# Where three stage seams of a two-layer decoder trunk norm and transpose their tiles, on eight cores

## The chip, the cores and the metric

The kernel runs on the 8 NeuronCores of one Trainium2 chip. Each core computes two of the 16 sequences, and the cores exchange nothing. A core has TensorE (PE, matrix products and transposes into PSUM), VectorE (DVE), ScalarE (ACT), GpSimd (POOL) and a sync engine (SP), each with a queue of its own that runs in program order; semaphores order them against each other. The metric is the device time of the slowest core in microseconds.

## The reference

The reference computes a trunk of two layers over `x` (16 x 2048 x 1024). Cut to what is computed:

```python
for i in range(2):
    h = rms_norm(x, mix_norm_g[i])
    # layer 0: gMLP gating + stick-breaking attention; layer 1: retention, 4 heads
    x = x + (hybrid_sg_sb_mixer(h, ...) if i % 2 == 0 else retention_mixer(h, ...))
    x = x + conv_ffn(rms_norm(x, ffn_norm_g[i]), ffn_w_up[i], ffn_conv_w[i], ffn_conv_b[i], ffn_w_down[i])
    gate = sigmoid(rms_norm(x, ple_norm_g[i]) @ ple_w_gate[i])
    x = x + gate * rms_norm(p[i] @ ple_w_proj[i], ple_post_g[i])
return rms_norm(x, final_norm_g)
# conv_ffn: a = h @ w_up; causal depthwise conv of width 3 over positions; (gelu(gate) * up) @ w_down
```

## The kernel before

A core keeps the residual stream X of one sequence in SBUF, as 16 tiles of 128 tokens by 1024, and runs six stages over it for each of its two sequences: mixer 0, FFN 0, embedding stage 0 (the gate with `p`, called PLE in the code), mixer 1 (retention), FFN 1, embedding stage 1, which is also the final norm and writes the output ("final stages" below).

**Norming a tile** has two halves. `norm_h` (L449, ACT) copies a tile of X, scaled by its reciprocal root mean square, to a bf16 buffer. `norm_tr` transposes it in 8 pieces of 128 x 128 on TensorE into one PSUM bank (L458), and DVE multiplies it by the gain and writes it to SBUF (L462, "gain multiply"). `norm_hT2` does both. The statistics come from `stat_tile`: a Square with accumulation on ACT (L435) and two small operations on POOL (L429, L431).

**FFN** (`phase_ffn_ple`, L1081 ff.). The up product runs over 22 column chunks, and each chunk over five stretches of 410 tokens; one such item has 16 matmuls (L1168) into two of six PSUM banks, two ACT copies (L1174, L1176), four conv steps on DVE (L1178 to L1185), a Gelu on ACT (L1182) and a product on POOL (L1187). In front of an item `make_ht` norms all tiles up to three beyond those that the item reads, with two buffers and banks 6 and 7 in turn. So seven tiles are normed before item 0, and three before each of the items 1, 2 and 3. The down product of each quarter of the chunks is spread over the items of the next quarter (L1134, added to X by DVE in L1141, "adds"); the last quarter's goes into the embedding stage.

**Embedding stage.** The loop over `m` runs 16 + 7 times. An iteration issues, for tile m-1, `norm_tr`; for m, the last down product (10 matmuls into banks 6 and 7); for m-3, `act_gate` (Square over the projection L1278, Sigmoid of the gate L1280), POOL's statistics, the embedding multiply on DVE (`u_of`, L1283) and POOL's product (`prod`, L1288); for m the adds and `stat_tile`; for m-4 the residual update on DVE (`xfin`, L1238) and the Square of the result (L435; L1246 in final stages); in final stages for m-6 the output (L1251); for m-2 the gate product (L1263, 16 matmuls, banks 2 and 3) and the projection (L1271, 4 matmuls, banks 4 and 5); for m `norm_h`. Iterations 16 to 22 drain the loop. The scheduler lets no second engine read a PSUM bank before the first reader has finished with it, so L1283 waits for L1278.

**Retention** (`phase_mix1`). Four heads with 16 steps each. A step of `stage_a` has the q/k product (L1421, 32 matmuls), four rotary multiplies on DVE (L1430) and POOL's sums (L1433, L1434); L1451 is the v and gate product, L1525 the transposes of the head's output Y. Before step 0, DVE scales four pieces of the output weights (L1380) and the tiles 0 and 1 are normed with one buffer; in head 0, step i norms tile i+2, with bank 3.

**Order and memory.** Nothing reorders work: each engine runs its instructions as the Python code emits them. The scheduler (`Sched.add`) only puts in the waits that reads and writes need. SBUF is one arena, and a buffer placed over old ones waits for all their readers and writers.

## Time and profile before

| | before |
|---|---|
| median of 3 runs | 5250.73 us (5227.94 to 5593.7) |
| profiled execution | 5247.87 us, its span on the slowest core 5246.0 us |
| spans of the other cores | 5203.1 to 5232.6 us |
| mean granted TensorE clock, core 0 | 0.940 |
| PE, DVE, ACT, POOL busy | 84%, 61%, 47%, 29% of the span |

The run of 5593.7 us was disturbed; the two others and the profiled one are comparable. In timelines, a row gives the start and the length in us, the engine, the line of the kernel, the operation with destination and source, how many there are, and in brackets how long the engine stood before it and what ended that. PE rows come from a pipelined engine, so the lengths of neighbouring rows overlap a little. The granted clock is given in parts of 2.4 GHz; 0.5 is 1.2 GHz.

### The profile page before, as it was taken

Reading aid. Unit: us, or ns where it says so; the run is one execution under the profiler, and the core shown is the slowest. Engines: PE = TensorE matmul, PEld = TensorE weight load, DVE = VectorE, ACT = ScalarE, POOL = GpSimd, SP = SyncE. Lnnn points to the kernel's source line nnn. Section 1 sums busy time; section 2 is a strip of 40 time slices with the busy share of each in tenths; the row PEclk is TensorE's granted clock in tenths of the full one; section 3 lists DMA queues with packets and bytes.
Section 4 is the critical chain, followed back from the end, with each engine's and each line's share of the span. In section 5 each row is a group of like instructions: output and inputs, shape, how many; then the busy total and the mean of one; then the engine's idle time right before and its main releaser. Section 6 shows DMA issues by size and latency. Waiting matters only on the chain.

```text
span 5246.0 us, 78294 instructions; the slowest of 8 cores (5203.1 to 5246.0 us)
## 1 busy us (share of the span) xinstructions
PE 4428.8 (84%) x25713; PEld 2227.8 (42%) x26098; DVE 3188.2 (61%) x5552; ACT 2474.1 (47%) x3578; POOL 1505.9 (29%) x1899
## 2 busy tenths in 40 slices
PE   4887789987789897998758877899878889889986
PEld 2322245543445454554323222455435555445542
DVE  3333477765666666776643334777656666677766
ACT  3787644345322235433547875543453222354444
POOL 1112222225222232222521122222252222322225
PEclk9998889999899998999979988999999999989998
DMA  5001032331221111222330010222302220122111
GB/s 127 9 9 25 1 45 41 45 51 18 52 45 31 31 28 29 41 45 52 95 84 9 9 25 1 49 37 45 62 15 45 46 47 15 27 39 44 35 37 65
DMA packets 110862, 204.28 MB, mean 39 GB/s; under 512 B 48896, under 2 KB 82048, under 8 KB 103808
## 3 DMA queue, kind: packets, MB, share of 16 engines
q0 software_dynamic: 21456, 132.29, 14.8%
q1 hardware_dynamic: 89008, 66.96, 5.0%
q8 instruction: 216, 3.54, 0.3%
q14 instruction: 182, 1.49, 0.1%
HBM read 304.24 MB, written 16.78 MB: 61 GB/s over the span
## 4 chain that ended last, share of the span: by engine, by line
PE 57%; DVE 14%; ACT 13%; issue 6%; DMA 6%; POOL 3%; DVEq 0%; ACTq 0%; POOLq 0%; SPq 0%
PE pbig L1168 18%; PE pbig L1134 11%; PE pbig L1451 8%; PE pbig L591 7%; PE pbig L1421 4%; DVE arena L1543 3%; DMA arena<-consts 3%; DVE arena L1430 2%; ACT arena L778 2%; ACT arena L1174 2%; DVE arena L1178 2%; PE pbig L800 2%; ACT arena L814 2%; PE pbig L802 2%; ACT arena L449 2%
## 5 line engine op out<-in xcount | busy, mean ns | idle before, releaser
L1168 PE MATMUL pbig<-arena 128*128 128x412 bf16 (+1 forms) x7040 | 1274.5, 341 | 0.7 <-DMA arena<-ffn_w_up 0.7
L1168 PEld LDWEIGHTS pbig<-arena 128*128 128x128 bf16 x7040 | 693.7, 99 | 563.8 <-issue 23.5
L1187 POOL TENSOR_TENSOR arena<-arena 128x410 bf16<-128x410 f32 (+1 forms) x440 | 463.8, 1054 | 1315.7 <-DVE arena L1185 1197.9
L1134 PE MATMUL pbig<-arena 128*128 128x512 bf16 x2680 | 671.4, 398 | 36.2 <-DVE arena L1141 16.4
L591 PE MATMUL pbig<-arena 128*128 128x512 bf16 x1719 | 478.4, 412 | 143.7 <-DMA arena<-arena 97.5
L1174 ACT ACTIVATE arena<-pbig,arena 128x410 f32<-128x410 f32 (+1 forms) x440 | 304.6, 692 | 546.0 <-PE pbig L1168 545.8
L1451 PE MATMUL pbig<-arena 128*128 128x512 bf16 x2046 | 475.5, 386 | 61.0 <-DVE arena L1543 60.9
L1178 DVE SCALAR_TENSOR_TENSOR arena<-pbig,arena 128x410 f32<-128x410 f32 (+1 forms) x440 | 283.8, 645 | 274.8 <-ACT arena L1174 252.6
L1182 ACT ACTIVATE arena<-arena 128x410 f32<-128x410 f32 (+1 forms) x440 | 240.0, 545 | 443.4 <-DVE arena L1180 443.4
L1134 PEld LDWEIGHTS pbig<-arena 128*128 128x128 bf16 x2816 | 282.9, 102 | 367.1 <-issue 95.0
L1503 ACT ACTIVATE arena<-arena 128x512 bf16<-128x512 f32 x240 | 147.2, 630 | 614.5 <-DVE arena L1500 578.8
L1141 DVE TENSOR_TENSOR arena<-pbig,arena 128x512 f32<-128x512 f32 x512 | 351.9, 687 | 99.4 <-PE pbig L1134 68.4
L462 DVE TENSOR_TENSOR arena<-pbig,arena 128x1024 bf16<-128x1024 bf16 x160 | 193.6, 1222 | 268.5 <-PE pbig L458 268.0
L435 ACT ACTIVATE arena<-arena 128x1024 bf16<-128x1024 f32 x160 | 169.1, 1057 | 389.8 <-DVE arena L1141 237.2
L778 ACT ACTIVATE arena<-pbig 128x1024 bf16<-128x1024 f32 (+2 forms) x320 | 269.7, 896 | 175.6 <-PE pbig L802 122.9
L786 DVE TENSOR_TENSOR arena<-arena 128x1024 bf16<-128x1024 bf16 (+3 forms) x256 | 172.2, 673 | 294.8 <-ACT arena L778 239.8
L814 ACT ACTIVATE arena<-pbig 128x1024 bf16<-128x1024 f32 (+1 forms) x320 | 274.9, 894 | 133.8 <-PE pbig L826 128.3
L458 PE MATMUL pbig<-arena 128*128 128x128 bf16 x1280 | 126.9, 258 | 248.6 <-ACT arena L449 232.8
L591 PEld LDWEIGHTS pbig<-arena 128*128 128x128 bf16 x1792 | 168.0, 103 | 370.8 <-issue 235.8
L1430 DVE TENSOR_TENSOR arena<-pbig,arena 128x256 f32<-128x256 f32 x512 | 181.6, 417 | 234.6 <-PE pbig L1421 182.0
L1451 PEld LDWEIGHTS pbig<-arena 128*128 128x128 bf16 x2048 | 194.6, 99 | 300.6 <-issue 96.2
L1180 DVE SCALAR_TENSOR_TENSOR arena<-pbig,arena 128x410 f32<-128x410 f32 (+1 forms) x440 | 283.6, 645 | 47.2 <-DVE arena L1178 1.8
(118 smaller groups left out, 6778.4 us busy)
## 6 DMA issues: line engine op xcount, KB each, us to landing
arena<-ffn_w_up POOLq DMA_DIRECT2D x88, 512.0 KB, 5.3
arena<-ret_w_in POOLq DMA_DIRECT2D x8, 3072.0 KB, 23.7
arena<-x SPq DMA_DIRECT2D x32, 512.0 KB, 6.5
arena<-consts SPq DMA_DIRECT2D x128, 128.0 KB, 2.3
out<-arena SPq DMA_DIRECT2D x32, 512.0 KB, 4.0
arena<-ffn_w_down POOLq DMA_DIRECT2D x8, 1536.0 KB, 14.3
arena<-ab_w_in POOLq DMA_DIRECT2D x10, 1024.0 KB, 25.4
arena<-ffn_w_down POOLq DMA_DIRECT2D x8, 1280.0 KB, 11.3
```

What stands on the lines that cost most here:

```text
L591: ins = e.matmul(pb[b][:], lhsT=lhs(kc), rhs=rhs(kc), start=(kc == 0), stop=(kc == 7))
L778: S.add("act", lambda e: e.activation(out=dst, in_=src, func=AF.Softplus), reads=tsrc, writes=[TSP[x]])
L814: S.add("act", lambda e: e.activation(out=AW[q][:, :, c0:512], in_=src, func=AF.Exp), reads=pT(wpair(n)), writes=[TAW[q]])
L1134: ins = e.matmul(pb[b][:], lhsT=GT[pp][:, cc, m * 128:(m + 1) * 128], rhs=WDN[pp][:, cc, n2 * 512:(n2 + 1) * 512], start=(cc == 0), stop=( ...
L1141: S.add("dve", (lambda e, b=b, n2=n2: e.tensor_tensor(out=k.X[:, m, n2 * 512:(n2 + 1) * 512], in0=pb[b][:], in1=k.X[:, m, n2 * 512:(n2 + 1 ...
L1168: ins = e.matmul(pb[b][:, 0:n + 2], lhsT=WUP[sl][:, kc, o:o + 128], rhs=HT[:, kc, t0:t0 + n + 2], start=(kc == 0), stop=(kc == 7))
L1174: S.add("act", (lambda e, G=G, tg=tg, c=c, n=n: e.activation(out=tg, in_=G[:, 0:n], func=AF.Identity, scale=cw(0, c), bias=cb(c))), reads= ...
L1178: S.add("dve", (lambda e, G=G, tg=tg, c=c, n=n: e.scalar_tensor_tensor(out=tg, in0=G[:, 1:n + 1], scalar=cw(1, c), in1=tg, op0=ALU.mult, o ...
L1180: S.add("dve", (lambda e, G=G, tg=tg, c=c, n=n: e.scalar_tensor_tensor(out=tg, in0=G[:, 2:n + 2], scalar=cw(2, c), in1=tg, op0=ALU.mult, o ...
L1187: S.add("pool", (lambda e, gg=gg, tu=tu, pp=pp, cc=cc, t0=t0, t1=t1: e.tensor_tensor(out=GT[pp][:, cc, t0:t1], in0=gg, in1=tu, op=ALU.mult ...
L1430: S.add("dve", (lambda e, ri=ri, xin=xin, tab=tab: e.tensor_tensor(out=rt[ri], in0=xin, in1=tab, op=ALU.mult)), reads=[pbT[0], Tcs[par]], ...
L1451: ins = e.matmul(pb[b][:], lhsT=HT[:, kc, tsl], rhs=W[:, kc, o:o + 512], start=(kc == 0), stop=(kc == 7))
```

## The change

Three edits, one for each kind of seam. First, `make_ht` in FFN issues `norm_h` up to two tiles ahead of `norm_tr`, with three buffers. Second, the embedding loop issues `norm_tr` of tile m-1 behind the down product, the adds and the statistics of tile m. Third, iterations 16 to 22 of layer 0's embedding loop each issue one `norm_tr` of a tile for retention (tiles 0 to 6) and `norm_h` one tile ahead of it; retention's tile buffer HT1 and two buffers `hn1` are placed for this at the arena's base, over GT1 and WDN1. Retention then finds tiles 0 to 6 normed, and its head 0 norms tile 7 in step 0 to tile 15 in step 8, with the copy one tile ahead. Its other buffers move by up to 4 KB; no operation is added or removed.

```diff
-    hn2, Thn2 = A.ring_bf(1024, "hnf", 2)
+    hn2, Thn2 = A.ring_bf(1024, "hnf", 3)
...
     def make_ht(upto):
         while ht_next[0] <= min(upto, NT - 1):
             i = ht_next[0]
-            norm_hT2(k, i, gcol, hn2[i % 2], Thn2[i % 2], 6 + (i % 2), HT[:, :, 2 + i * 128:2 + (i + 1) * 128], THT[i])
+            while nh_next[0] <= min(i + 2, NT - 1):
+                y = nh_next[0]
+                norm_h(k, y, hn2[y % 3], Thn2[y % 3])
+                nh_next[0] += 1
+            norm_tr(k, gcol, hn2[i % 3], Thn2[i % 3], 6 + (i % 2), HT[:, :, 2 + i * 128:2 + (i + 1) * 128], THT[i])
             ht_next[0] += 1
...
     for m in range(NT + 7):
         ok = lambda i: 0 <= i < NT
-        if ok(m - 1):
-            c_ = (m - 1) % 2
-            norm_tr(k, gcol, hn[c_], Thn[c_], c_, hT[c_], ThT[c_])
         if ok(m):
             down_mm(m, 1, 3, 6, 7)
...
         if ok(m):
             down_add(m, 6, 7)
             stat_tile(k, m, ring)
+        if ok(m - 1):
+            c_ = (m - 1) % 2
+            norm_tr(k, gcol, hn[c_], Thn[c_], c_, hT[c_], ThT[c_])
         if ok(m - 4):
             xfin(m - 4)
             fin_stat(m - 4)
...
         if ok(m):
             norm_h(k, m, hn[m % 2], Thn[m % 2])
+        if not final and m >= NT and "mix1" in k.stages:
+            if m == NT:
+                mix1_ht(k)
+            k.pre_head.step()
     k.stats_ready = not final
...
+def mix1_ht(k):
+    A = k.A
+    w = k.pre_head
+    HT, w.THT = A.bf(8 * SEQ, "HT1", NT, at=k.base)
+    w.HT = r3(HT, SEQ)
+    w.ht = True
+    hb, thb = A.ring_bf(1024, "hn1", 2, at=k.base + 32 * KB)
+    w.hn = hb, thb
+    w.nh, w.nt = 0, 0
+    gcol = VFM["mix_g"] + 8
+
+    def step():
+        while w.nh < min(w.nt + 2, NT):
+            norm_h(k, w.nh, hb[w.nh % 2], thb[w.nh % 2])
+            w.nh += 1
+        i = w.nt
+        norm_tr(k, gcol, hb[i % 2], thb[i % 2], i % 2, w.HT[:, :, i * 128:(i + 1) * 128], w.THT[i])
+        w.nt += 1
+    w.step = step
...
-    hn, Thn = A.bf(1024, "hn1")
-    jk, Tjk = A.ring_bf(1024, "junk1", 1)
+    jk, Tjk = hn1, Thn1
...
-    for i in range(2):
-        norm_hT2(k, i, gcol, hn, Thn, 3, HT[:, :, i * 128:(i + 1) * 128], THT[i])
+    while w.nt < 2:
+        w.step()
...
-        if h == 0 and i + 2 < NT:
-            norm_hT2(k, i + 2, gcol, hn, Thn, 3, HT[:, :, (i + 2) * 128:(i + 3) * 128], THT[i + 2])
+        if h == 0 and w.nt < NT:
+            x = w.nt
+            while w.nh < min(x + 2, NT):
+                norm_h(k, w.nh, hn1[w.nh % 2], Thn1[w.nh % 2])
+                w.nh += 1
+            norm_tr(k, gcol, hn1[x % 2], Thn1[x % 2], 3, HT[:, :, x * 128:(x + 1) * 128], THT[x])
+            w.nt += 1
```

The order of instructions on the engines, where it moves. Lines of after are 5 higher up to FFN, and 37 or so higher in retention; L435, L449, L458 and L462 are the same in both.

ACT, start of FFN 0, from the last work of mixer 0 on: L449 are the norm copies, L1174 and L1176 (after: L1179 and L1181) the two copies of an item, L1182 (L1187) its Gelu. Before:

```order
L449 ACTIVATE arena<-arena 128x1024 x7
L1174 ACTIVATE arena<-pbig,arena 128x410
L1176 ACTIVATE arena<-pbig,arena 128x410
L1182 ACTIVATE arena<-arena 128x410
L449 ACTIVATE arena<-arena 128x1024 x3
L1174 ACTIVATE arena<-pbig,arena 128x410
L1176 ACTIVATE arena<-pbig,arena 128x410
L1182 ACTIVATE arena<-arena 128x410
L449 ACTIVATE arena<-arena 128x1024 x3
```

After:

```order
L449 ACTIVATE arena<-arena 128x1024 x9
L1179 ACTIVATE arena<-pbig,arena 128x410
L1181 ACTIVATE arena<-pbig,arena 128x410
L1187 ACTIVATE arena<-arena 128x410
L449 ACTIVATE arena<-arena 128x1024 x3
L1179 ACTIVATE arena<-pbig,arena 128x410
L1181 ACTIVATE arena<-pbig,arena 128x410
L1187 ACTIVATE arena<-arena 128x410
L449 ACTIVATE arena<-arena 128x1024 x3
```

Nine copies instead of seven lie ahead of item 0; the groups of three behind the Gelus of items 0 and 1 hold copies of tiles two further on, and behind item 2's Gelu one is left instead of three.

TensorE, embedding stage of layer 0, its iterations 1 to 3: L1134 (L1139) is the down product, L458 the transposes, L1263 (L1268) the gate product, L1271 (L1276) the projection. Before:

```order
L458 MATMUL pbig<-arena 128x128 x8
L1134 MATMUL pbig<-arena 128x512 x10
L458 MATMUL pbig<-arena 128x128 x8
L1134 MATMUL pbig<-arena 128x512 x10
L1263 MATMUL pbig<-arena 128x512 x16
L1271 MATMUL pbig<-arena 128x512 x4
L458 MATMUL pbig<-arena 128x128 x8
L1134 MATMUL pbig<-arena 128x512 x10
L1263 MATMUL pbig<-arena 128x512 x16
L1271 MATMUL pbig<-arena 128x512 x4
```

After:

```order
L458 MATMUL pbig<-arena 128x128 x8
L1139 MATMUL pbig<-arena 128x512 x10
L458 MATMUL pbig<-arena 128x128 x8
L1268 MATMUL pbig<-arena 128x512 x16
L1276 MATMUL pbig<-arena 128x512 x4
L1139 MATMUL pbig<-arena 128x512 x10
L458 MATMUL pbig<-arena 128x128 x8
L1268 MATMUL pbig<-arena 128x512 x16
L1276 MATMUL pbig<-arena 128x512 x4
```

The transposes stand between the down product and the gate product instead of ahead of both. DVE at the same place, two iterations: L462 is the gain multiply, L1283 (L1288) the embedding multiply, L1141 (L1146) the adds, L1238 (L1243) the residual update. Before:

```order
L462 TENSOR_TENSOR arena<-pbig,arena 128x1024
L1283 TENSOR_TENSOR arena<-pbig,arena 128x1024
L1141 TENSOR_TENSOR arena<-pbig,arena 128x512 x2
L1238 SCALAR_TENSOR_TENSOR arena<-arena 128x1024
L462 TENSOR_TENSOR arena<-pbig,arena 128x1024
L1283 TENSOR_TENSOR arena<-pbig,arena 128x1024
L1141 TENSOR_TENSOR arena<-pbig,arena 128x512 x2
L1238 SCALAR_TENSOR_TENSOR arena<-arena 128x1024
```

After:

```order
L1288 TENSOR_TENSOR arena<-pbig,arena 128x1024
L1146 TENSOR_TENSOR arena<-pbig,arena 128x512 x2
L462 TENSOR_TENSOR arena<-pbig,arena 128x1024
L1243 SCALAR_TENSOR_TENSOR arena<-arena 128x1024
L1288 TENSOR_TENSOR arena<-pbig,arena 128x1024
L1146 TENSOR_TENSOR arena<-pbig,arena 128x512 x2
L462 TENSOR_TENSOR arena<-pbig,arena 128x1024
L1243 SCALAR_TENSOR_TENSOR arena<-arena 128x1024
```

The gain multiply stands between the adds and the residual update instead of ahead of the embedding multiply.

TensorE, from the last two gate products of that stage into retention's step 0, where L1421 (L1453) is the q/k product and L1465 (L1502) follows on it. Before:

```order
L1263 MATMUL pbig<-arena 128x512 x16
L1271 MATMUL pbig<-arena 128x512 x4
L1263 MATMUL pbig<-arena 128x512 x16
L1271 MATMUL pbig<-arena 128x512 x4
L458 MATMUL pbig<-arena 128x128 x16
L1421 MATMUL pbig<-arena 128x128 x32
L458 MATMUL pbig<-arena 128x128 x8
L1465 MATMUL pbig<-arena 128x128 x2
```

After:

```order
L1268 MATMUL pbig<-arena 128x512 x16
L1276 MATMUL pbig<-arena 128x512 x4
L458 MATMUL pbig<-arena 128x128 x8
L1268 MATMUL pbig<-arena 128x512 x16
L1276 MATMUL pbig<-arena 128x512 x4
L458 MATMUL pbig<-arena 128x128 x48
L1453 MATMUL pbig<-arena 128x128 x32
L458 MATMUL pbig<-arena 128x128 x8
L1502 MATMUL pbig<-arena 128x128 x2
```

One tile's transposes have moved between the two gate products, and six tiles' (48 transposes) instead of two stand ahead of the first q/k product.

## Rows read from the trace of the kernel before

**Rows 1.** List of waits: engine, line, waited for; us in total, times, longest us

```profile
PE pbig L458 <- ACT arena L449: 232.8, 113, 9.9
```

**Rows 2.** Windows: stretch, length, busy us of each engine (instructions), clock, DMA

```profile
685.45:722.57 37.12, 21.62 (x121) 12.93 (x122) 18.30 (x21) 16.32 (x19) 3.15 (x3) 0.68 0.44 71
1199.86:1209.06 9.20, 7.08 (x38) 3.29 (x39) 5.90 (x5) 5.25 (x9) 5.13 (x7) 1.00 0.01 3
1180.18:1291.63 111.45, 90.56 (x452) 41.67 (x459) 69.08 (x60) 63.13 (x96) 61.00 (x82) 0.95 0.12 22
2494.09:2610.57 116.48, 92.08 (x453) 42.37 (x459) 80.38 (x70) 64.24 (x96) 68.86 (x83) 0.94 0.33 93
```

**Rows 3.** Timeline, TensorE, FFN start: start, us, engine line operation, [idle before <-releaser]

```profile
682.50 2.95 PE L1168 MATMUL pbig<-arena 128*128 128x412 bf16 x16 [0.56 <-DMA arena<-ffn_w_up]
690.86 2.05 PE L458 MATMUL pbig<-arena 128*128 128x128 bf16 x16 [5.41 <-ACT arena L449]
...
694.26 4.77 PE L1168 MATMUL pbig<-arena 128*128 128x412 bf16 x16
...
706.53 3.76 PE L1168 MATMUL pbig<-arena 128*128 128x412 bf16 x16
```

**Rows 4.** Timeline, DVE, FFN start: last conv step of item 1

```profile
701.97 0.65 DVE L1185 SCALAR_TENSOR_TENSOR arena<-pbig,arena 128x410 f32<-128x410 f32 x1
```

**Rows 5.** Timeline, TensorE, embedding loop: transposes of one iteration

```profile
1199.86 0.61 PE L458 MATMUL pbig<-arena 128*128 128x128 bf16 x8 [2.11 <-ACT arena L449]
```

**Rows 6.** Timeline, ACT, embedding loop: one period

```profile
1198.59 1.13 ACT L449 ACTIVATE arena<-arena 128x1024 bf16<-128x1024 f32 x1
1199.63 1.00 ACT L1278 ACTIVATE arena<-pbig 128x1024 bf16<-128x1024 f32 x1
1200.53 0.19 ACT L1278 ACTIVATION_READ_ACCUMULATOR arena<-pbig 128x1 f32 x1
1200.62 1.01 ACT L1280 ACTIVATE arena<-pbig 128x1024 f32<-128x1024 f32 x1
...
1206.73 1.06 ACT L435 ACTIVATE arena<-arena 128x1024 bf16<-128x1024 f32 x1 [1.16 <-DVE arena L1238]
...
1207.79 1.13 ACT L449 ACTIVATE arena<-arena 128x1024 bf16<-128x1024 f32 x1
```

**Rows 7.** Timeline, DVE, embedding loop: one period

```profile
1200.58 1.23 DVE L462 TENSOR_TENSOR arena<-pbig,arena 128x1024 bf16<-128x1024 bf16 x1 [3.19 <-PE pbig L458]
1201.72 1.21 DVE L1283 TENSOR_TENSOR arena<-pbig,arena 128x1024 f32<-128x1024 f32 x1
1202.85 1.48 DVE L1141 TENSOR_TENSOR arena<-pbig,arena 128x512 f32<-128x512 f32 x2
1204.24 2.34 DVE L1238 SCALAR_TENSOR_TENSOR arena<-arena 128x1024 f32<-128x1024 f32 x1
```

**Rows 8.** Timeline, POOL, embedding loop

```profile
1203.14 2.36 POOL L1288 TENSOR_TENSOR arena<-arena 128x1024 f32<-128x1024 f32 x1 [1.37 <-DVE arena L1283]
1205.73 0.90 POOL L429 TENSOR_SCALAR arena<-arena 128x1 f32<-128x1 f32 x1 [0.23 <-ACT arena L435]
```

**Rows 9.** Timeline, TensorE: the first projection of an embedding stage

```profile
1171.63 1.16 PE L1271 MATMUL pbig<-arena 128*128 128x512 bf16 x4 [2.59 <-DMA arena<-pT]
```

**Rows 10.** Timeline, ACT: the last Square of the embedding stage

```profile
1315.32 1.06 ACT L435 ACTIVATE arena<-arena 128x1024 bf16<-128x1024 f32 x1 [2.50 <-DVE arena L1238]
```

**Rows 11.** Timeline, TensorE: retention's first q/k product, and a transpose in step 1

```profile
1321.06 3.62 PE L1421 MATMUL pbig<-arena 128*128 128x128 bf16 x32
...
1335.14 0.61 PE L458 MATMUL pbig<-arena 128*128 128x128 bf16 x8 [1.99 <-ACT arena L449]
```

**Rows 12.** Timeline, TensorE, head 0: transposes of Y, once a step

```profile
1463.35 0.39 PE L1525 MATMUL pbig<-arena 128*128 128x128 bf16 x4
...
1473.59 0.39 PE L1525 MATMUL pbig<-arena 128*128 128x128 bf16 x4
...
1482.88 0.39 PE L1525 MATMUL pbig<-arena 128*128 128x128 bf16 x4
```

More of the change, by code:

```diff
@@ L1116, in phase_ffn_ple @@
     ht_next = [0]
+    nh_next = [0]
     def make_ht(upto):
@@ L1333, in mix1_prefetch @@
     w.alloc, w.load_head = alloc, load_head
+    w.ht = None
     alloc(0, k.base + O_Z)
@@ L1345, in phase_mix1 @@
     A.top = k.base
-    HT, THT = A.bf(8 * SEQ, "HT1", NT)
-    HT = r3(HT, SEQ)
+    if w.ht is None:
+        mix1_ht(k)
+    HT, THT = w.HT, w.THT
+    (hn1, Thn1) = w.hn
+    A.top = k.base + 36 * KB
     w.alloc(1, None)
```

## The prediction

> **What bounds the kernel now.** I read the page first: TensorE is the busiest engine and the one that ends last, but its share is an average over stages. So I went to the list of waits for what it waits on in the places that the change touches. One entry carries them: the transposes of the normed tiles (L458) wait 232.8 us in all for the ACT copy that makes a normed tile (L449), 113 times [rows 1]. Then I cut out three kinds of stretch with the windows view and followed each in the timelines, engine by engine.
>
> The start of an FFN stage [rows 2 to 4]: from the end of the first up product (690.86 less its idle 5.41 is 685.45) to the end of the fourth at 722.57, 37.12 us pass, and TensorE is busy in 21.62 of them at a granted clock of 0.68. In front of item 1 it stands for 5.41 us, and from the end of product 1 (694.26 and 4.77: 699.03) to the start of product 2 at 706.53 pass 7.50, since norm copies lie in ACT's queue behind the previous item's Gelu. There are four such stages.
>
> The embedding loop, one iteration per token tile [rows 2, 5 to 8]: a period is 9.20 us, of which TensorE is busy 7.08, and it stands 2.11 in front of the transposes. Between the norm copies of m=3 and m=15 (12 periods) 111.45 us pass in a layer-0 stage and 116.48 in a final one: 9.29 and 9.71 each. No engine is full; a chain closes on itself. I read it from starts: norm copy 1198.59, transposes 1199.86 (+1.27), gain multiply L462 1200.58 (+0.72), embedding multiply L1283 1201.72 (+1.14), down adds L1141 1202.85 (+1.13), residual update L1238 1204.24 (+1.39), its Square on ACT 1206.73 (+2.49), next norm copy 1207.79 (+1.06). The sum is 9.20.
>
> The start of retention [rows 10 to 12]: the first q/k product starts at 1321.06, after two tiles normed behind the last Square of the embedding stage; then head 0 takes 10.24 us for a step with a transpose (1463.35 to 1473.59) and 9.29 for one without (1473.59 to 1482.88).
>
> **Edit 1, FFN tiles two ahead.** Of the three tiles in front of an item, two copies are now ahead of the previous Gelu. Their transposes run into the old idle; the third still waits, for its own copy and, in its PSUM bank, for the gain multiply of the tile two before it, which DVE does after the previous item's four conv steps. Item 1: the third transpose starts where the first did, 5.41 after the product; the product used to follow 3.40 later (690.86 to 694.26), now some 0.8: 2.6 less. Items 2 and 3: the conv steps end at 702.62, which is 3.6 after the product's end at 699.03; a multiply of 1.14 follows, the transpose starts at 4.85, the product at 5.5 to 5.6, against 7.50 before: 1.9 to 2.0 less. Together 6.5 us a stage. The clock sets the bounds: a product took 2.95 us at 682.50, but 4.77 and 3.76 behind the stands. If all three came at 2.95, some 4.5 more would be won; if all came at the lower level, 1.2 GHz, twice 2.95, some 3 would be lost. TensorE still stands 3 to 4 us in front of each third transpose, so I keep the clock as it is: 6.5, bounds 3.5 to 11. Four stages: **26 us** (14 to 44). The two additional copies ahead of item 0 lie beside its product and cost nothing; without that cover they would cost 1 us each.
>
> **Edit 2, embedding transposes behind the down products.** TensorE: down product, transposes, gate, projection. DVE: embedding multiply, adds, gain multiply, residual update. The obvious reading is that the 2.11 of idle goes and the loop becomes TensorE's, 7.1 us. I do not take it, because the chain is shortened and not opened. The Square over the projection (L1278) is behind the norm copy in ACT's queue, and the embedding multiply waits for that Square; after it the same chain runs on. Let N be the norm copy's start. The Square starts at N+1.04, its accumulator read ends at N+2.13 (1200.53 and 0.19), so the embedding multiply can start at about N+2.2 instead of 3.13. Adds N+3.4, gain multiply N+4.8, residual update N+5.9. POOL's product (L1288) starts 1.42 after the embedding multiply and lasts 2.36, so it ends at N+6.0; before, the residual update, begun at 1204.24 while that product ran, ended at 1206.58, 1.08 after the product's end at 1205.50 [rows 7, 8]. Again so: N+7.1. Square N+7.25, next norm copy N+8.3. The row of before that is missing is the gain multiply beside POOL's product, which the new order brings: N+4.8 lies inside the product. The nearest are the adds, also with one operand from PSUM: the two took 1.48 us from 1202.85 on, while the product ran, and were not held up. Taken so, the multiply costs 1.14 and the sum stands. If it were held until N+6.0 as the update was, the next norm copy would come at N+9.6, and 48 periods would cost 14 to 19 us instead of giving 45. The Trainium skill's page "SBUF — State Buffer", section "Who interferes with whom", has a rule for it: a VectorE instruction with two SBUF inputs and a GpSimd one that reads SBUF exclude each other, and the first to issue wins; one with a single SBUF input outside the two-port modes does not contend. By that rule, too, the sum is 8.3, and the trace agrees in both halves (2.34 us for the update, 1.48 for the adds).
>
> So a period of 8.3 replaces 9.2, and what leaves the chain is the way over TensorE (0.9); the gain multiply stays on it, only later. The stall moves too: the gate product now follows the transposes at once, and its banks are read until N+3.04 by the Sigmoid that starts at 1200.62, so TensorE stands about 1.3 us there. With 7.1 of work in 8.3 it has room, and its slow stretches (clock 0.95 over the 12 periods, which is 0.09 of the 9.29) are covered. Layer-0 stages: 12 x (9.29 - 8.31) = 11.7; final stages lose the same 0.9 of 9.71, 10.8. Twice each: **45 us**. Before m=3 there is nothing to win, though the first transposes no longer hold up the down products: the first projection waits for the pT load in any case [rows 9], and the loads are issued where they were. The tail after m=15 is the old one. Bounds: 0, if another link binds at the old period, and 4 x 12 x (9.5 - 7.1) = 115 if TensorE binds.
>
> **Edit 3, retention's tiles in the drain.** Seven tiles instead of two are normed before the first q/k product. Tiles 0 to 3 fit into ACT's and TensorE's idle in the drain; tiles 4 to 7 stand behind the last Square (1315.32) and go at 1.2 us each, so the product starts about 1321.5 against 1321.06. Two gain multiplies lie in front of embedding multiplies, one of them in front of the last: 0.4 later. Head 0 then has nine steps with a transpose instead of fourteen: 5 x 0.95 = 4.8. The 1.99 us in front of the transposes at 1335.14 goes; of it I take 1.2 (bounds 0 and 1.99), since the rotary multiplies lie in front of the gain multiply on DVE. 4.8 + 1.2 - 0.4 = 5.6, call it 6, twice: **12 us** (4 to 18). The shorter waits before later transposes bring nothing, for the same reason. The constant loads on SP's queue now wait for other dead buffers, at the latest for POOL's last product, as they did.
>
> **Sum.** 26 + 45 + 12 = 83 us. The profiled execution took 5247.87 us (span 5246.0); the median of three is 5250.73. 5247.87 - 83 = 5165, taken as 5164, that is 1.6% less.
>
> **Rivals.**
> A, TensorE binds in the embedding loop at 7.1 to 7.2 us. For it: its idle of 2.11 is what the trace names. Against it: the loop over L1278, L1283, L1141, L462, L1238, Square, norm copy needs no TensorE and sums to 8.3. It would save about 110 there: 5248 - 26 - 110 - 12 = 5100.
> B, the loop keeps its period, since the stall only goes from the transposes to the gate product behind the Sigmoid. For it: that wait is new. Against it: it is 1.3 us in a loop with 1.2 to 2.1 of room. 5248 - 38 = 5210.
> C, the other side: the product on POOL and the residual update on DVE change places. If the update starts first, the product waits until N+7.1 and ends at N+9.5; the statistics of tile m stand behind it on POOL (they lie behind it now, stretched to 0.90 while DVE holds on [rows 8]), so the norm copy comes at about N+10.5, 1.3 later than before: 48 x 1.3 = 62, and 5248 + 62 - 38 = 5272. It decides if the product starts later than N+5.9. It needs the Sigmoid (N+3.04) and the embedding multiply (N+3.4), so there are 2.5 us to spare. What the Trainium skill's page "SBUF — State Buffer" says of the order of issue, in that section, is this case with its signs turned.
> D, edit 1 or edit 3 does nothing, as the third transpose and the last Square bind: 5190 and 5176, inside the range.
>
> **How the numbers follow.** Forecast 0.74 (with D in it; 5135 to 5195 by the bounds of the terms and an execution's own spread), A 0.08, B 0.12, C 0.04, the rest 0.02. The range 5125 to 5215 holds the forecast and B and leaves A and C out. The line at 2%, about what a measurement of this kernel can tell from no change, is 5146. Below it are A, about a tenth of the forecast and half of the rest: faster 0.16. C is 0.5% slower, so slower by over 2% is 0.02 at most, and within 2% is 0.82.
>
> **What would show it.** The norm copies of the embedding loop 8.3 us apart (8.8 in final stages), with TensorE's idle in front of the gate product and named after the Sigmoid; 7.1 apart would be A, 9.2 B, above 10 C, with the product on POOL begun after the residual update. In the FFN start, 31 us from the end of the first up product to the end of the fourth instead of 37, with one wait before each third transpose. In retention, a first q/k product no earlier than before relative to the last Square, and nine steps of 10.2 us in head 0. The prediction is wrong if the first projection no longer waits for pT, if the granted clock in the FFN start goes to 0.5 or to 1.0, or if the drain's additional copies delay the last Square by more than 1 us.

## The result and the profile after

| | before | after |
|---|---|---|
| comparable runs | 5227.94, 5236.03, 5250.73 us | 5166.85, 5173.64, 5178.73, 5180.23 us |
| ratio after to before | | 0.9879, interval 0.9847 to 0.9911 (47 to 80 us less) |
| profiled span, slowest core | 5246.0 us | 5165.0 us |
| mean of the 8 cores' spans | 5225 us | 5145.5 us |
| PE busy; mean clock of core 0 | 84%; 0.940 | 86%; 0.948 |

Runs in which one half of the chip showed a lower granted clock and took longer are left out of this and of every ratio below, and where a trace is of such a run, it is read on a core of the other half. The time fell by 1.2%. The two profiled executions lie 81 us apart, since before's stood at the upper end of its runs and after's at the lower.

Windows of the kernel after, core 0: stretch, length, busy us of PE, PEld, DVE, ACT and POOL, clock, DMA. The first is the FFN start, from the ACT copy of item 0 to that of item 3; the second is one period of the embedding loop; the two last are 12 periods, layer 0 and final. They answer to [rows 2].

```profile
689.94:720.14 30.20, 17.53 (x121) 10.83 (x119) 17.92 (x21) 14.02 (x17) 3.15 (x3) 0.83 0.50 84
1203.84:1212.22 8.38, 7.08 (x40) 3.33 (x39) 4.84 (x5) 5.25 (x10) 5.36 (x7) 1.00 0.00 1
1178.55:1279.49 100.94, 88.31 (x461) 41.13 (x459) 58.27 (x60) 63.11 (x97) 63.62 (x82) 0.97 0.13 23
2466.66:2574.05 107.39, 87.81 (x463) 40.53 (x461) 70.02 (x70) 64.23 (x97) 72.09 (x83) 1.00 0.34 99
```

The FFN start took 37.16 us before, read in the same way, and takes 30.20. The 12 periods took 111.45 and 116.48, and take 100.94 and 107.39. The list of waits of after, with the entry of [rows 1] and the two that took part of its place:

```profile
PE pbig L458 <- ACT arena L449: 74.5, 44, 5.6
...
PE pbig L1268 <- ACT arena L1285: 70.0, 52, 2.6
...
PE pbig L458 <- DVE arena L462: 40.6, 22, 4.1
```

The same two in before:

```profile
PE pbig L1263 <- ACT arena L1280: 15.5, 9, 2.3
PE pbig L458 <- DVE arena L462: 13.7, 22, 1.6
```

232.8 us of waiting for the norm copy became 74.5, which is 158.3 less. Of these, 54.5 us are found again in front of the gate product, behind the Sigmoid, and 26.9 in front of transposes that wait for a gain multiply. About half of the wait had moved elsewhere, and 81 us were won.

Timeline of after, TensorE at the FFN start (columns as in [rows 3]):

```profile
686.90 2.95 PE L1173 MATMUL pbig<-arena 128*128 128x412 bf16 x16 [1.38 <-DMA arena<-ffn_w_up]
689.68 1.06 PE L458 MATMUL pbig<-arena 128*128 128x128 bf16 x16
695.25 1.01 PE L458 MATMUL pbig<-arena 128*128 128x128 bf16 x8 [4.51 <-ACT arena L449]
696.06 3.96 PE L1173 MATMUL pbig<-arena 128*128 128x412 bf16 x16
699.86 1.06 PE L458 MATMUL pbig<-arena 128*128 128x128 bf16 x16
704.99 1.01 PE L458 MATMUL pbig<-arena 128*128 128x128 bf16 x8 [4.08 <-DVE arena L462]
705.80 4.21 PE L1173 MATMUL pbig<-arena 128*128 128x412 bf16 x16
```

Two tiles' transposes follow their product at once, and the third waits: for its copy in front of item 1, and in front of item 2 for the gain multiply that empties its bank.

One period of the embedding loop after, timeline of all engines in order of time, to be laid beside [rows 5 to 8]:

```profile
1203.84 1.13 ACT L449 ACTIVATE arena<-arena 128x1024 bf16<-128x1024 f32 x1
...
1206.08 1.23 DVE L1288 TENSOR_TENSOR arena<-pbig,arena 128x1024 f32<-128x1024 f32 x1 [3.44 <-ACT arena L1283]
...
1207.03 3.61 PE L1268 MATMUL pbig<-arena 128*128 128x512 bf16 x16 [1.30 <-ACT arena L1285]
...
1207.22 1.48 DVE L1146 TENSOR_TENSOR arena<-pbig,arena 128x512 f32<-128x512 f32 x2
...
1207.51 2.36 POOL L1293 TENSOR_TENSOR arena<-arena 128x1024 f32<-128x1024 f32 x1 [0.49 <-DVE arena L1288]
...
1208.61 1.22 DVE L462 TENSOR_TENSOR arena<-pbig,arena 128x1024 bf16<-128x1024 bf16 x1
...
1209.74 1.28 DVE L1243 SCALAR_TENSOR_TENSOR arena<-arena 128x1024 f32<-128x1024 f32 x1
```

With N = 1203.84 the embedding multiply starts at N+2.24, the adds at 3.38, the gain multiply at 4.77, the residual update at 5.90 and the next copy at 8.38. The product on POOL ends at N+6.03, so two things come together at N+6: the chain through the gain multiply, and POOL's end.

The start of retention after, last Square, first q/k product, and two steps with a transpose and one without (before: [rows 10 to 12]):

```profile
1304.71 1.06 ACT L435 ACTIVATE arena<-arena 128x1024 bf16<-128x1024 f32 x1 [1.46 <-DVE arena L1243]
...
1312.38 3.57 PE L1453 MATMUL pbig<-arena 128*128 128x128 bf16 x32 [1.73 <-DVE arena L1412]
...
1391.45 0.39 PE L1562 MATMUL pbig<-arena 128*128 128x128 bf16 x4
1401.46 0.39 PE L1562 MATMUL pbig<-arena 128*128 128x128 bf16 x4
1411.47 0.39 PE L1562 MATMUL pbig<-arena 128*128 128x128 bf16 x4
1420.76 0.39 PE L1562 MATMUL pbig<-arena 128*128 128x128 bf16 x4
```

Square to product is 7.67 us, against 5.74 before. The steps are 10.01 and 9.29 apart.

### The profile page after: what moved, and what is told of

Read it like the earlier page. It is cut to its first block, busy times and chain, and to the rows that moved or that the text cites. A ratio compares the mean times of both kernels' runs of the same rounds, so it can differ in the third digit from the quotient of the medians.

```text
span 5165.0 us, 78931 instructions; the slowest of 8 cores (5116.3 to 5165.0 us)
## 1 busy us (share of the span) xinstructions
PE 4430.7 (86%) x26098; PEld 2212.5 (43%) x26098; DVE 3143.9 (61%) x5552; ACT 2471.6 (48%) x3578; POOL 1510.1 (29%) x1899
## 4 chain that ended last, share of the span: by engine, by line
PE 56%; DVE 13%; ACT 12%; issue 8%; DMA 6%; POOL 3%; DVEq 0%; ACTq 0%; POOLq 0%; SPq 0%
PE pbig L1173 18%; PE pbig L1139 9%; PE pbig L1488 8%; PE pbig L591 7%; PE pbig L1453 4%; DVE arena L1580 3%; DMA arena<-consts 3%; DVE arena L1462 2%; DMA arena<-pT 2%; ACT arena L778 2%; ACT arena L814 2%; PE pbig L800 2%; DVE arena L1183 2%; ACT arena L1179 2%; PE pbig L802 2%
## 5 line engine op out<-in xcount | busy, mean ns | idle before, releaser
L1139 PE MATMUL pbig<-arena 128*128 128x512 bf16 x2816 | 664.7, 387 | 25.4 <-DVE arena L1146 15.6
L591 PE MATMUL pbig<-arena 128*128 128x512 bf16 x1792 | 494.3, 413 | 130.1 <-DMA arena<-arena 95.9
L1179 ACT ACTIVATE arena<-pbig,arena 128x410 f32<-128x410 f32 (+1 forms) x440 | 304.3, 692 | 524.5 <-PE pbig L1173 524.0
L1488 PE MATMUL pbig<-arena 128*128 128x512 bf16 x2048 | 476.9, 387 | 60.7 <-DVE arena L1580 60.3
L1187 ACT ACTIVATE arena<-arena 128x410 f32<-128x410 f32 (+1 forms) x440 | 240.0, 545 | 442.2 <-DVE arena L1185 442.1
L1183 DVE SCALAR_TENSOR_TENSOR arena<-pbig,arena 128x410 f32<-128x410 f32 (+1 forms) x440 | 283.7, 645 | 273.7 <-ACT arena L1179 207.7
L1139 PEld LDWEIGHTS pbig<-arena 128*128 128x128 bf16 x2816 | 277.1, 99 | 361.2 <-issue 64.4
L1146 DVE TENSOR_TENSOR arena<-pbig,arena 128x512 f32<-128x512 f32 x512 | 351.9, 687 | 86.8 <-PE pbig L1139 52.7
L1268 PE MATMUL pbig<-arena 128*128 128x512 bf16 x1024 | 251.7, 403 | 94.5 <-ACT arena L1285 70.0
L435 ACT ACTIVATE arena<-arena 128x1024 bf16<-128x1024 f32 x160 | 169.0, 1056 | 307.9 <-DVE arena L1146 148.3
L1190 DVE SCALAR_TENSOR_TENSOR arena<-pbig,arena 128x410 f32<-128x410 f32 (+1 forms) x440 | 283.7, 645 | 47.8 <-DVE arena L1188 2.3
L1185 DVE SCALAR_TENSOR_TENSOR arena<-pbig,arena 128x410 f32<-128x410 f32 (+1 forms) x440 | 283.6, 645 | 47.5 <-DVE arena L1183 2.3
```

The costliest lines, as they stand in the source:

```text
L591: ins = e.matmul(pb[b][:], lhsT=lhs(kc), rhs=rhs(kc), start=(kc == 0), stop=(kc == 7))
L1139: ins = e.matmul(pb[b][:], lhsT=GT[pp][:, cc, m * 128:(m + 1) * 128], rhs=WDN[pp][:, cc, n2 * 512:(n2 + 1) * 512], start=(cc == 0), stop=( ...
L1146: S.add("dve", (lambda e, b=b, n2=n2: e.tensor_tensor(out=k.X[:, m, n2 * 512:(n2 + 1) * 512], in0=pb[b][:], in1=k.X[:, m, n2 * 512:(n2 + 1 ...
L1179: S.add("act", (lambda e, G=G, tg=tg, c=c, n=n: e.activation(out=tg, in_=G[:, 0:n], func=AF.Identity, scale=cw(0, c), bias=cb(c))), reads= ...
L1183: S.add("dve", (lambda e, G=G, tg=tg, c=c, n=n: e.scalar_tensor_tensor(out=tg, in0=G[:, 1:n + 1], scalar=cw(1, c), in1=tg, op0=ALU.mult, o ...
L1190: S.add("dve", (lambda e, U=U, tu=tu, c=c, n=n: e.scalar_tensor_tensor(out=tu, in0=U[:, 2:n + 2], scalar=cw(2, 22 + c), in1=tu, op0=ALU.mu ...
```

## The experiments

**The parts apart.** Three kernels hold one edit each; the fourth is the changed kernel again, on the same chip as they.

```diff
# e1_ffn: before with edit 1 only
+            while nh_next[0] <= min(i + 2, NT - 1):
...
+            norm_tr(k, gcol, hn2[i % 3], Thn2[i % 3], 6 + (i % 2), HT[:, :, 2 + i * 128:2 + (i + 1) * 128], THT[i])
# e2_ple: before with edit 2 only (norm_tr of m-1 behind stat_tile of m)
# e3_drain: before with edit 3 only (mix1_ht, k.pre_head.step() in iterations 16 to 22)
```

> Edit 1 alone on the kernel before: FFN's norm copies up to two tiles ahead, with three buffers. Theory (the sum by parts): the trace of the change shows 6.9 us less from the fourth part of an FFN start (30.2 instead of 37.2 from the first to the fourth product), so about 5248 - 27 = 5221, the embedding loops at their old 9.2 and 9.7 us a period. Rival (the parts are not additive, and the FFN's gain is only what the other edits moved): less than 10 us.

> Edit 2 alone on the kernel before: the transposes and the gain multiply behind the down product and the adds. Theory: periods of 8.4 and 9.0 us instead of 9.2 and 9.7, 38 us in all, about 5209. Rival (TensorE's idle is what the edit fills): the period goes to 7.1 and the time under 5160. Rival (the gain came from the shifted start of the loop): periods as before.

> Edit 3 alone on the kernel before: seven of retention's tiles normed in the drain. Theory: 12 to 16 us, about 5234: five steps of head 0 without transposes (5 x 0.95), eight steps shorter by 0.24, minus a first q/k product that starts 1.5 to 2 us later relative to the last Square. Rival (the drain is not idle enough): no gain, 5248 or more.

> The changed kernel again, beside its three parts on one chip. Theory: 5170, and its gain is the sum of the gains of the three parts within 15 us. Rival (the parts share an idle): the sum of the parts is over by more than 15 us.

| | ratio to before | us |
|---|---|---|
| edit 1 alone | 0.9953 (0.9935 to 0.9970) | -25 |
| edit 2 alone | 0.9920 (0.9899 to 0.9941) | -42 |
| edit 3 alone | 0.9991 (0.9971 to 1.0012) | -5, not told from nothing |
| all three | 0.9870 (0.9845 to 0.9895) | -68 |

The parts add up (72 against 68). In the traces each shows its own mark and no other: edit 1 alone has 28.8 us from the first up product to the fourth on core 4 (28.74 with all three, 35.06 before), edit 2 alone has periods of 8.38 and 8.96, edit 3 alone has the q/k product 7.56 us behind the last Square. FFN start and embedding loop thus came out near their size. The drain's 5 us can be told neither from nothing nor from the 12 that were forecast; the traces decide below.

**What holds the embedding loop.** Between after and the next two kernels the only difference is the place of the gain multiply, or the product on POOL, or both.

```diff
# e5_late: behind xfin and fin_out instead of ahead of them
-        if ok(m - 1):
-            c_ = (m - 1) % 2
-            norm_tr(k, gcol, hn[c_], Thn[c_], c_, hT[c_], ThT[c_])
         if ok(m - 4):
             xfin(m - 4)
...
+        if ok(m - 1):
+            c_ = (m - 1) % 2
+            norm_tr(k, gcol, hn[c_], Thn[c_], c_, hT[c_], ThT[c_])
# e7_noprod: after without this line; e6_late_noprod: e5_late without it
-            prod(m - 3)
```

> The changed kernel with one line moved: in the embedding loop the transposes of tile m-1 (and with them the gain multiply of 128 x 1024 on VectorE) stand behind the four adds of the final normalization instead of ahead of them, so that the gain multiply of 1.1 us is no longer between the down adds and the residual update. Theory (VectorE's residual update and GpSimd's product hold each other up, whichever comes first waits): the residual update then starts about 2.5 us behind the embedding multiply, runs into the GpSimd product of 2.3 us, and is held to that product's end, so that its end, and the Square behind it, come no earlier than now: the norm copies stay 8.3 to 8.5 us apart in the first layer and 8.8 to 9.0 in the last, and the residual update lengthens from 1.28 to about 2.3 us. Rival (the chain is only the sum of its operations): the copies come 1.1 to 1.2 us closer together, 7.2 us in the first layer, and the time falls by about 60 x 1.1 = 66 us to some 5110 us.

> The changed kernel with only the GpSimd product left out (the gate's multiplication is missing from what is computed). Theory: the chain of the embedding loop runs over the embedding multiply, the two down adds, the gain multiply, the residual update and the Square, and the product now ends just as the residual update starts, so that leaving it out gives little: the period falls from 8.38 by no more than 0.2 us (8.2 to 8.4). Rival (the product still sets the update's end): it falls by 1 us or more, to about 7.3.

> The same order as e5_late, and the GpSimd product (gate times embedding input) is left out: the gate's multiplication is missing from what is computed. Theory: with the product gone nothing holds the residual update, which takes 1.1 to 1.3 us, and the period of the embedding loop falls to 7.2 to 7.4 us in the first layer (TensorE's own 7.1 is next), some 60 x 1.1 us less than e5_late. Rival: if the product does not hold VectorE up, the period stays where e5_late has it.

Distance of norm copies in a settled loop, sequence 0, layer 0 and final, from the ACT timelines:

| | product on POOL in | product left out |
|---|---|---|
| gain multiply ahead of the update | 8.38, 8.96 (after) | 8.38, 8.96 (e7_noprod) |
| gain multiply behind the update | 8.31, 8.82 (e5_late) | 7.26, 8.17 (e6_late_noprod) |

Each of the two taken away alone gives 0 to 0.14 us, both together 1.12 in layer 0 and 0.79 in final stages. The one run of e5_late took 5165.5 us, as long as after's shortest (5166.85), and that of e6_late_noprod 5112.3; e7_noprod has no time that can be compared. The timeline of e5_late, DVE and POOL, shows what takes the gain multiply's place:

```profile
1196.85 1.23 DVE L1288 TENSOR_TENSOR arena<-pbig,arena 128x1024 f32<-128x1024 f32 x1 [2.30 <-ACT arena L1283]
...
1198.28 2.36 POOL L1293 TENSOR_TENSOR arena<-arena 128x1024 f32<-128x1024 f32 x1 [0.49 <-DVE arena L1288]
...
1199.38 2.33 DVE L1243 SCALAR_TENSOR_TENSOR arena<-arena 128x1024 f32<-128x1024 f32 x1
```

The update starts 1.1 us sooner after the embedding multiply than in after, while POOL's product runs (until 1200.64), and ends at 1201.71, 1.07 behind it: 2.33 us long, as the 2.34 of [rows 7]. (The expectation has it that whichever comes first waits; in every row here it is the one that starts second.) In e6_late_noprod the same update, with no product, takes its own time:

```profile
1203.51 3.61 PE L1268 MATMUL pbig<-arena 128*128 128x512 bf16 x16 [0.17 <-ACT arena L1285]
...
1205.08 1.28 DVE L1243 SCALAR_TENSOR_TENSOR arena<-arena 128x1024 f32<-128x1024 f32 x1
```

TensorE stands 0.17 us instead of 1.3 there: it is the next limit, near its 7.08 of work. So the rival of the prediction in which TensorE binds was barred by two chains of equal length, not by one.

**Opening the chain.** If both chains end in the Square behind the residual update, the update has to leave them. e8_order does that without leaving work out: a tile's update comes at the end of the iteration that made its product, and not in the next one, and its Square has a place of its own, ahead of the Square behind the adds.

```diff
# e8_order
         if ok(m - 3):
...
             prod(m - 3)
+        if ok(m - 4):
+            fin_sq(m - 4)
...
         if ok(m - 1):
...
+        if ok(m - 3):
+            rstd_of(k, ssp, rsp, Tssp[m - 3], Trsp[m - 3], m - 3)
         if ok(m - 4):
-            xfin(m - 4)
-            fin_stat(m - 4)
-        if final and ok(m - 6):
-            fin_out(m - 6)
+            fin_rstd(m - 4)
+        if ok(m - 3):
+            xfin(m - 3)
+        if final and ok(m - 5):
+            fin_out(m - 5)
```

> The changed kernel with another order inside the embedding loop: the transposes of tile m-1 with their gain multiply stay behind the down adds, the Square of the final statistics of tile m-4 stands ahead of the down adds' statistics, and the residual update of tile m-3 comes an iteration earlier than now, at the end of its own iteration, behind the gain multiply. What it is for: the next tile's Square on ScalarE then waits for the down adds only, not for a residual update. Theory: the period falls from 8.38 to about 7.2 us in the first layer (TensorE's 7.1 then binds) and from 8.9 to about 8.2 in the last, where ScalarE has more to do; about 30 x 1.1 + 30 x 0.7 = 54 us, less some at the ends, so 45 us below the changed kernel, near 5125 to 5130. Rival (the lock between VectorE and GpSimd moves to the next pair): the period stays at 8.0 or more and the gain is under 20 us.

The period is 7.31 in layer 0 and 8.50 in final stages; the ratio is 0.9804 (0.9767 to 0.9841), 35 us below the changed kernel, where 45 were expected. Such a distance, here and below, is the difference of two ratios to before, the changed kernel's of 0.9870 and this one, taken on two chips; both intervals together leave it uncertain by some 20 us either way. Timeline of e8_order, DVE, POOL, ACT and TensorE (lines from L1273 on are 5 higher than in after):

```profile
1203.83 3.61 PE L1273 MATMUL pbig<-arena 128*128 128x512 bf16 x16 [0.23 <-ACT arena L1290]
...
1204.30 2.37 POOL L1298 TENSOR_TENSOR arena<-arena 128x1024 f32<-128x1024 f32 x1 [1.01 <-DVE arena L1293]
...
1205.40 1.22 DVE L462 TENSOR_TENSOR arena<-pbig,arena 128x1024 bf16<-128x1024 bf16 x1
...
1205.64 1.06 ACT L435 ACTIVATE arena<-arena 128x1024 bf16<-128x1024 f32 x1 [0.92 <-DVE arena L1146]
...
1209.20 1.28 DVE L1243 SCALAR_TENSOR_TENSOR arena<-arena 128x1024 f32<-128x1024 f32 x1 [2.58 <-POOL arena L431]
```

The update now runs 2.5 us behind the product's end (1206.67) and is not held, and TensorE stands 0.23 us. The gain multiply at 1205.40 lies wholly inside the product and takes 1.22, which is the row that the prediction missed. The edit also moved a Square and POOL's statistics, so the 35 us belong to the new order as a whole. In final stages an additional DVE instruction of 1.28 us, the output's, comes between update and embedding multiply; 8.2 was expected and 8.50 measured.

**The drain's bank.**

```diff
# e12_bank, in mix1_ht's step
-        norm_tr(k, gcol, hb[i % 2], thb[i % 2], i % 2, w.HT[:, :, i * 128:(i + 1) * 128], w.THT[i])
+        norm_tr(k, gcol, hb[i % 2], thb[i % 2], 6 + i % 2, w.HT[:, :, i * 128:(i + 1) * 128], w.THT[i])
```

> The changed kernel with the transposes of retention's first tiles, which are made in the last iterations of the first layer's embedding loop, in the PSUM banks 6 and 7 (free there) instead of 0 and 1. Theory: the first q/k product writes bank 0, and waits for the gain multiply that empties the last drained tile's transposes out of it; with other banks it starts 1.2 to 1.7 us earlier, 6.0 to 6.5 us behind the last Square of the embedding loop instead of 7.67. Rival (something else, such as the weights or the last product of the loop, holds it): it stays within 0.3 us of 7.67. For the whole time 3 us are expected, which one look cannot show.

ACT's last Square and TensorE's first q/k product in e12_bank:

```profile
1298.95 1.06 ACT L435 ACTIVATE arena<-arena 128x1024 bf16<-128x1024 f32 x1 [1.46 <-DVE arena L1243]
...
1303.88 1.01 PE L458 MATMUL pbig<-arena 128*128 128x128 bf16 x8 [0.54 <-DVE arena L462]
1304.68 2.53 PE L1453 MATMUL pbig<-arena 128*128 128x128 bf16 x32
```

The product follows the last transposes without a wait, 5.73 us behind the Square instead of 7.67, a little more than expected. The wait was the bank: the row of after names L1412, the scaling of output weights that follows the last gain multiply in DVE's queue, but here the product starts at 1304.68 while that scaling starts at 1306.14. (The one run took 5160.5 us; the 4 us of two stages are less than one run can show.)

**The rest of the FFN start.** In after, the third transposes in front of items 2 and 3 wait since their bank is emptied by a multiply behind the previous item's conv steps. e9_ffnafter asks for the tiles earlier.

```diff
# e9_ffnafter
-    make_ht(3)
+    make_ht(6)
...
-                make_ht(tiles[-1] + 3)
...
+                make_ht(tiles[-1] + 6)
```

> The changed kernel with FFN's first seven tiles normed at its start, and each later group's tiles normed behind, not ahead of, the up product of the group before, so that TensorE does not stand for the transposes' bank between the first up products. Theory: the transposes of tile 4 and on wait for a gain multiply that queues behind the convolution's work on VectorE; asked for earlier, they cost nothing, and the first four up products span 17 to 22 us instead of 30; four such starts give up to 35 to 50 us. Rival (VectorE's own work for the groups binds the start, so the wait moves to the next product): the first eight products take as long as now and the time stays within 10 us.

The removed call stood ahead of an item's up product, the new one stands behind it. Ratio 0.9801 (0.9777 to 0.9825), 36 us below the changed kernel. Timeline of e9_ffnafter, TensorE (L1172 is the up product):

```profile
684.66 2.95 PE L1172 MATMUL pbig<-arena 128*128 128x412 bf16 x16 [1.21 <-DMA arena<-ffn_w_up]
687.45 1.06 PE L458 MATMUL pbig<-arena 128*128 128x128 bf16 x16
689.99 0.61 PE L458 MATMUL pbig<-arena 128*128 128x128 bf16 x8 [1.49 <-DVE arena L462]
690.44 2.95 PE L1172 MATMUL pbig<-arena 128*128 128x412 bf16 x16
...
696.41 0.61 PE L458 MATMUL pbig<-arena 128*128 128x128 bf16 x8 [2.14 <-ACT arena L449]
696.86 2.95 PE L1172 MATMUL pbig<-arena 128*128 128x412 bf16 x16
...
703.11 1.01 PE L458 MATMUL pbig<-arena 128*128 128x128 bf16 x8 [2.41 <-DVE arena L462]
703.92 6.38 PE L1172 MATMUL pbig<-arena 128*128 128x412 bf16 x29
```

The fourth product starts 19.26 us after the first, instead of 28.74 in after. Part of it is clock: items 1 and 2 take 2.95 us each, in after 3.96 and 4.21, in before 4.77 and 3.76 [rows 3], and the stands ahead of the transposes are 1.5 to 2.4 us instead of 4.1 to 4.5.

**Retention's tables.** Three times a sequence DVE's rotary multiply waits for the load of cosine and sine. From the lists of waits of before and of after, of the whole span:

```profile
DVE arena L1430 <- DMA arena<-consts: 52.6, 6, 11.5
...
DVE arena L1462 <- DMA arena<-consts: 42.2, 6, 9.0
```

```diff
# e10_cs: three buffers for the tables; item n uses buffer n % 3
-    cs, Tcs = A.ring_f32(256, "cs", 2)
+    cs, Tcs = A.ring_f32(256, "cs", 3)
```

> The changed kernel with three buffers instead of two for retention's rotary tables. In the changed kernel VectorE's rotary multiply waits 8.5 us for the load of the tables once a head, in the items in which the next head's weights are being loaded. Theory: the load waits for its buffer and then queues behind the weights; with a third buffer it is issued an item (about 9.3 us) earlier and arrives in time: most of 8.5 us for each of 3 heads in 2 sequences, 25 to 50 us in all. Rival (the tables are late because the queues are full of the weights' packets, not because of when they are asked for): the wait only shrinks by a few us, and the time by under 15 us.

Ratio 0.9802 (0.9769 to 0.9835), 36 us below the changed kernel. The entry is gone from the list of waits. From the last Square over the projection to FFN's first up product pass 648.7 us in sequence 0 instead of 675.6 in after, where the list counts 26.0 of this wait in that stretch. The 128 table loads themselves, from issue to landing, in after and in e10_cs:

```profile
DMA to landing us min/median/max: 2.1/2.3/25.5
...
DMA to landing us min/median/max: 2.1/2.3/24.9
```

So the rival's cause is there, though not the outcome that it expected. The load was slow, and it is as slow as before in e10_cs. In after, the one that DVE waits for was issued at 1355.31, behind the loads of the next head's weights (3 MB at 1351.19 and 1 MB at 1351.82, on POOL's queue), and landed at 1380.78, 0.19 us behind the second of them; the wait ended at 1380.88. In e10_cs the load that meets the weights takes 24.3 us as well, but it was asked for a step earlier against its use, so nothing waits for it. The third buffer hides the slow load and does not shorten it.

**All of it.**

> The orders of e8_order and e9_ffnafter, the three table buffers of e10_cs and the banks of e12_bank together in the changed kernel: the best version that the readings point to. Expected from the sum of the parts: 45 + 35 + 25 us and a few below the changed kernel, about 5065 us (5030 to 5110). Rival (the parts bring nothing, as their own rivals say): 5150 or more.

e11_all (e8_order, e9_ffnafter, e10_cs and e12_bank in one kernel) has a ratio of 0.9608 (0.9575 to 0.9640) to before: about 5033 us, 205 less than before, some 137 less than the changed kernel and 32 less than the 5065 expected. The three timed parts make 107 us of it and the bank 4; the other 26 are within what the intervals leave open. It is faster than both kernels.

## Why the prediction was right, and where it was not

5164 us were forecast; the comparable runs of after have a median of 5176.2, and the profiled span is 5165.0. The time lies in the stated range, and it fell by less than 2%, as forecast. Part of that hit is luck of the base: the 83 us were taken from an execution of 5247.87, while the median of before's comparable runs is 5236. By spans of one execution each the change gave 81, by the timed ratio 63 (47 to 80), so that 83 is just outside. By segments between fixed marks in the two traces (core 0):

| | forecast | traces |
|---|---|---|
| four FFN starts, ACT copies of item 0 to item 3 | 26 | 22.8 |
| from there to the norm copy of m=3 in the embedding loop, four times | 0 | 4.0 |
| 48 embedding periods, m=3 to m=15 | 45 | 38.7 |
| from m=15 to FFN's first norm copy, twice (drain and retention) | 12 | 15.0 |
| rest of the span | 0 | 0.5 |

- **FFN start: right mechanism, size a little too large, and uneven.** 6.5 us a stage were forecast; the four stages gave 7.0, 6.1, 3.5 and 6.3. The stated releaser of items 2 and 3, the bank's gain multiply, is the one in the rows. Taking the clock "as it is" did little harm in the first stage: it rose from 0.68 to 0.83 in the stretch, and of the 6.96 us some 1.0 came from shorter products and 6.0 from the gaps between them. In the third stage the granted clock was 0.74 after and 0.76 before, the products of items 1 and 2 took 5.47 and 4.97 us instead of 4.17 and 3.66, which took back 2.6 us.
- **Embedding loop: right mechanism, size 6 us too large.** The chain's links came where they were put (N+2.24 for 2.2, 3.38 for 3.4, 4.77 for 4.8, 5.90 for 5.9). What was mis-sized is the end of the update. It was taken to be held until 1.08 us behind POOL's product, as in [rows 7, 8], which would be N+7.11; it started only 0.13 us before the product's end and ran its own 1.28 us from 5.90: N+7.18 for 7.1. That is 0.07 a period in layer 0 of sequence 0; in sequence 1 the settled period is 8.45. In final stages the forecast carried the 0.9 over from layer 0, to 8.8; the period is 8.96, and e5_late, in which the update is held, has 8.82. (What makes a final period longer than one in layer 0 is told below.)
- **The wait that moved was foreseen:** 1.30 us in front of the gate product, named after the Sigmoid, where 1.3 was said.
- **The residual update and the product on POOL.** The forecast rested on the row that the adds were not held while the product ran, and took the gain multiply to be like them. Rows in after (1208.61) and e8_order (1205.40) show it: 1.22 us inside the product. The Trainium skill's page "SBUF — State Buffer", section "Who interferes with whom", has it so: outside the two-port modes, a VectorE instruction with at most one SBUF input does not contend with GpSimd. The rows agree, and with the other half too (two SBUF inputs contend with a GpSimd instruction that reads SBUF): the update, with both inputs in SBUF, took 2.34 and 2.33 us beside the product and 1.28 without it.
- **Why TensorE did not bind.** The forecast's reason, a loop without TensorE that sums to 8.3, is right but was half of it. The table of four kernels above shows a second one of the same length, over POOL's product. Whoever had found only the first and moved the gain multiply would have won 0.07 us a period.
- **Retention: about 5 us instead of 12, and the rest is luck.** 15.0 us were measured, but 10.4 of them are the tables' wait, which went from 52.6 to 42.2 us on core 0 and which the forecast did not count. The same two numbers on the other cores leave 3.1 to 7.8 us for the two stages (retention and drain gave 6.6 to 23.1 us, and the wait fell by 2.2 to 16.3). That agrees with the 5 us of the edit alone. The tables' wait differs from execution to execution as well (32.0 us on core 0 in the second trace of the changed kernel); what set it was not separated.
- **The first q/k product.** "0.4 later" was said. The drain's last Square came 25.2 and 26.5 us behind the copy of m=15 in the two sequences, against 23.7 before, and the product 1.9 more behind it, because tile 6 was transposed into bank 0, which the q/k product writes. The text had counted copies and multiplies but not banks. A delay of the last Square by more than 1 us was named as a sign that the prediction is wrong, and it came: 1.5 and 2.8 us. The drain's copies are not all of it. "The tail after m=15 is the old one" was wrong: with edit 2 alone the first Square of the drain comes 7.18 us behind that copy, as with all three, against 5.63 before. For the last Square edit 2 alone has 23.6 to 24.9 (cores 4 and 5) and edit 3 alone 23.6 to 25.2 (cores 0 and 4); the shares were not separated.
- **The later steps.** "The shorter waits before later transposes bring nothing" was wrong in the good direction: steps with a transpose take 10.01 us instead of 10.24. The idle time in front of those transposes is gone with it, which fits, though nothing tested it alone.
- **A slip in the bounds.** If the three products after the first all ran at 1.2 GHz, by their lengths of 4.77, 3.76 and 5.01 us some 4 us a stage would be lost, not 3. The forecast does not hang on it.

## What to carry to other kernels

When a wait moves in a loop without a full engine, write the whole cycle down in starts, and then look for a second cycle of the same length before taking the next link out: two chains that meet in one instruction give nothing singly and all of it together. An instruction that another engine's instruction holds up belongs where that other one is idle, not where its own engine is: the order that has the update away from the product gave 35 us, and shortening the way to the update 0.07 us a period. Where tiles are made ahead of time, count the PSUM banks that they leave behind like any other buffer. A small load that is asked for behind big ones can take ten times its usual time; one more buffer, which asks for it a step earlier, hides that.

## What the runs showed of the hardware

Tiny POOL operations on 128x1 are held up as well. In after, final stage, POOL beside DVE:

```profile
2516.97 1.28 DVE L1243 SCALAR_TENSOR_TENSOR arena<-arena 128x1024 f32<-128x1024 f32 x1
...
2517.32 0.97 POOL L429 TENSOR_SCALAR arena<-arena 128x1 f32<-128x1 f32 x1 [0.30 <-ACT arena L435]
...
2518.16 1.28 DVE L1256 SCALAR_TENSOR_TENSOR arena<-arena 128x1024 f32<-128x1024 f32 x1
...
2518.44 1.41 POOL L431 TENSOR_TENSOR arena<-arena 128x1 f32<-128x1 f32 x1
...
2519.94 1.15 ACT L449 ACTIVATE arena<-arena 128x1024 bf16<-128x1024 f32 x1 [0.40 <-POOL arena L431]
```

The same two operations take 0.19 and 0.55 us when DVE is not in such an instruction. Here they end 0.04 and 0.41 us behind a DVE instruction, and the norm copy waits for the second: it starts 1.55 us behind the Square of the final statistics (L1251, at 2518.39), where layer 0, in which it waits for no POOL operation, has 1.06 [rows 6]. That is 0.49 of the 0.58 us by which a final period is longer.

The wait for retention's tables differs between cores that run the same program: 42.2 us on core 0 and 30.6 on core 4 in after, and 29.7 on core 0 and 56.3 on core 6 in e8_order. A stall on a late load of shared data is then also a spread between cores, and the slowest core sets the time. How much of e8_order's shortfall (35 for 45 us) it made was not separated.
